# Attention scores from high and low halves in three one-pass products, roots of x for eight tiles at a time, and the last addition of q's rotation on GpSimd

## The reference

```python
q = rope(rmsnorm(q.reshape(B, L, N_HEADS, HEAD_DIM), q_norm_w), pos)
k = rope(rmsnorm(k.reshape(B, L, N_KV_HEADS, HEAD_DIM), k_norm_w), pos)
s = jnp.einsum('bnqkgd,bnskd->bnkgqs', qb, kc).astype(jnp.float32) / math.sqrt(HEAD_DIM)
p = sink_softmax(s, mask[None, :, None, None], sinks).astype(vc.dtype)
o = jnp.einsum('bnkgqs,bnskd->bnqkgd', p, vc)
```

## Time and profile before

| | before |
|---|---|
| median of three runs | 1855.61 us |
| profiled execution, own time | 1853.68 us |
| its span, first to last instruction | 1851.9 us |
| TensorE matmuls busy | 1766.0 us (95%) |
| TensorE weight loads busy | 1428.1 us (77%) |
| VectorE busy | 1230.6 us (66%) |
| ScalarE busy | 647.7 us (35%) |
| GpSimd busy | 428.7 us (23%) |
| mean granted TensorE clock | 0.974 of full speed |

### The profile page before, as it was taken

How to read it: one execution, slowest core, us unless ns; L and a number is a source line. 1 busy time by engine, 2 the same in 40 slices (tenths; PEclk the granted TensorE clock), 3 DMA queues, 4 the chain that set the end, 5 groups by cost and what they waited for, 6 DMA issues and landing times. The chain is left out here.

```text
span 1851.9 us, 26031 instructions
## 1 busy us (share of the span) xinstructions
PE 1766.0 (95%) x8822; PEld 1428.1 (77%) x8822; DVE 1230.6 (66%) x2862; ACT 647.7 (35%) x1682; POOL 428.7 (23%) x554
## 2 busy tenths in 40 slices
PE   5899999999999996999999997999979999999999
PEld 4677777777777774888888885777757888888886
DVE  5787888677877877666656535898646564566532
ACT  5454455445445445231122102454332212122210
POOL 1122222122222222000000034799701111111110
PEclk8999999999999997999999998999988999999999
DMA  7211221123221101333342043666564455354322
GB/s 254 83 61 61 69 82 61 61 63 117 102 87 64 38 25 55 103 96 134 100 143 78 24 152 98 161 173 165 127 146 116 108 131 159 117 136 113 117 92 65
DMA packets 198403, 191.61 MB, mean 103 GB/s; under 512 B 121344, under 2 KB 157184, under 8 KB 198272
## 3 DMA queue, kind: packets, MB, share of 16 engines
q1 hardware_dynamic: 187968, 181.53, 33.1%
q10 hardware_dynamic: 10304, 8.43, 2.2%
HBM read 130.81 MB, written 59.10 MB: 103 GB/s over the span
## 5 line engine op out<-in xcount | busy, mean ns | idle before, releaser
L1028 PE MATMUL ps_b<-b_WH,b_XH 128*128 128x512 f32 (+1 forms) x792 | 292.8, 370 | 18.7 <-DVE b_WL L1370 12.2
L1030 PE MATMUL ps_b<-b_WH,b_XL 128*128 128x512 f32 (+1 forms) x792 | 283.0, 357 | 0.0
L1029 PE MATMUL ps_b<-b_WL,b_XH 128*128 128x512 f32 (+1 forms) x792 | 282.8, 357 | 0.0
L1028 PEld LDWEIGHTS ps_b<-b_WH,b_XH 128*128 128x128 f32 x792 | 151.3, 191 | 48.4 <-issue 25.1
L1030 PEld LDWEIGHTS ps_b<-b_WH,b_XL 128*128 128x128 f32 x792 | 151.0, 191 | 22.2
L982 POOL TENSOR_TENSOR b_XL<-b_XT,b_XH 128x1024 fp32r<-128x1024 f32 x33 | 79.9, 2422 | 375.6 <-ACT b_XH L1200 316.8
L1029 PEld LDWEIGHTS ps_b<-b_WL,b_XH 128*128 128x128 f32 x792 | 151.7, 191 | 19.1
L1266 ACT ACTIVATE b_SM<-ps_b,b_small 128x128 f32<-128x128 f32 x256 | 113.7, 454 | 109.4 <-DVE b_small L1441 106.9
L674 PE MATMUL ps_e<-w_X0H,w_nextH 128*128 128x464 f32 x320 | 122.2, 382 | 1.6 <-DVEq L719 1.6
L676 PE MATMUL ps_e<-w_X0H,w_nextL 128*128 128x464 f32 x320 | 120.0, 375 | 0.0
L675 PE MATMUL ps_e<-w_X0L,w_nextH 128*128 128x464 f32 x320 | 119.7, 374 | 0.0
(11 more groups left out here) (316 smaller groups left out, 4084.6 us busy)
## 6 DMA issues: line engine op xcount, KB each, us to landing
b_XT<-in_xb SPq DMA_DIRECT2D x33, 512.0 KB
b_XR<-in_x SPq DMA_DIRECT2D x33, 512.0 KB, 4.7
w_XT<-in_xt SPq DMA_DIRECT2D x36, 464.0 KB, 7.2
l_X<-in_xr SPq DMA_DIRECT2D x32, 512.0 KB, 4.7
out_out<-l_OUT SPq DMA_DIRECT2D x32, 512.0 KB, 3.0
scr_gs<-e_TG SPq DMA_DIRECT2D x36, 232.0 KB, 2.0
scr_u<-w_ST SPq DMA_DIRECT2D x12, 696.0 KB, 3.7
g_U<-scr_u SPq DMA_DIRECT2D x192, 43.5 KB
```

The costliest lines, as they stand in the source:

```text
L1028: pe.matmul(bank[:, 0:c1 - c0], XH[b][:, k, :], WH[:, k, c0:c1], start=(k == 0), stop=False)
L1029: pe.matmul(bank[:, 0:c1 - c0], XH[b][:, k, :], WL[:, k, c0:c1], start=False, stop=False)
L1030: mm = pe.matmul(bank[:, 0:c1 - c0], XL[b][:, k, :], WH[:, k, c0:c1], start=False, stop=(k == KD - 1))
```

## The change

- Scores: QT and KT become pairs QTH, QTL and KTH, KTL of type fp32r. ScalarE writes the high halves (queries, keys), VectorE the low ones (new low_q, low_k), placed behind gate_attn(t). The 8 score matmuls of a tile become 24: high with high, low q with high k, high q with low k, into the same place in PSUM. TensorE waits for q's low half behind the first four and for k's behind the next four.
- Roots of x: x_rsqrt covers eight tiles and is called at t = 3, 11, 19, 27 instead of 3, 7, ..., 27. Loads and squares of x run ten tiles ahead instead of five, two a tile until t = 4.
- q's rotation: its addition moves from VectorE to GpSimd (rotated_q), between add_up(t-1) and low_x(t+2). k's stays on VectorE.
- Semaphore counts follow.

```diff
 def batch_of(t):
-    return 0 if t < 5 else (t - 5) // 4 + 1
+    return (t + 3) // 8
+
+def squares(t):
+    return range(t + 5 + min(t, 5), min(t + 6 + min(t + 1, 5), NT))
...
-                    if t + 5 < NT:
-                        load_xr(t + 5)
+                    for n in squares(t):
+                        load_xr(n)
...
+                def rotated_q(t):
+                    rope.wait(pool, tile(t), 3)
+                    pool.tensor_tensor(RQK[:, 0:DA], RQK[:, 0:DA], ZS[:, 0:DA], ALU.add).then_inc(q_rot, 1)
...
                 for t in range(NT):
                     if t >= 2:
                         add_up(t - 1)
+                    if t + 1 < NT:
+                        rotated_q(t + 1)
                     if t + 2 < NT:
                         low_x(t + 2)
                         tables(t + 2)
...
-                    for j in range(4):
-                        for g in HALVES:
-                            rows = slice(HD * g, HD * g + HD)
-                            mm = pe.matmul(ps[:, 4 + 2 * g + j // 2, 256 * (j % 2):256 * (j % 2) + 256], QT[rows, j, :], KT[rows, :, :],
-                                           start=True, stop=True)
-                            if j == 3:
-                                mm.then_inc(sc_full, 1)
+                    for i in range(2):
+                        for n, (q_, k_) in enumerate(((QTH, KTH), (QTL, KTH), (QTH, KTL))):
+                            if i == 0 and n == 1:
+                                pe.wait_ge(qT_lo, t)
+                            if i == 0 and n == 2:
+                                pe.wait_ge(kT_lo, t + 1)
+                            for j in (i, i + 2):
+                                for g in HALVES:
+                                    rows = slice(HD * g, HD * g + HD)
+                                    mm = pe.matmul(ps[:, 4 + 2 * g + j // 2, 256 * (j % 2):256 * (j % 2) + 256], q_[rows, j, :], k_[rows, :, :],
+                                                   start=(n == 0), stop=(n == 2))
+                                    if j == 3 and n == 2:
+                                        mm.then_inc(sc_full, 1)
...
                 def q_transposes(t):
-                    rope.wait(pe, tile(t), 4)
+                    pe.wait_ge(q_rot, t + 1)
...
                 def x_rsqrt(n):
-                    c = slice(0, 5) if n == 0 else slice(4 * n + 1, 4 * n + 5)
+                    c = slice(max(8 * n - 3, 0), min(8 * n + 5, NT))
...
+                    if part == 0:
+                        rope.mark(dve.tensor_tensor(r, z, cos, ALU.mult))
+                    else:
+                        rope.link(dve, tile(t), dve.tensor_tensor(r, z, cos, ALU.mult))
+                        rope.link(dve, tile(t), dve.tensor_tensor(RQK[:, c], RQK[:, c], ZS[:, c], ALU.add))
...
+                def low_q(t):
+                    dve.wait_ge(qT_out, t)
+                    if t >= 2:
+                        dve.wait_ge(sc_full, 2 * (t - 1))
+                    dve.tensor_tensor(QTL[:].rearrange("p j q -> p (j q)"), TB, QTH[:].rearrange("p j q -> p (j q)").bitcast(F32), ALU.subtract).then_inc(qT_lo, 1)
+
+                def low_k(t):
+                    dve.wait_ge(kT_out, t + 1)
+                    if t >= 2:
+                        dve.wait_ge(sc_full, 2 * (t - 1))
+                    dve.tensor_tensor(KTL[:, t % 2, :], KTB, KTH[:, t % 2, :].bitcast(F32), ALU.subtract).then_inc(kT_lo, 1)
...
                     if t:
                         gate_attn(t)
+                    if t + 1 < NT:
+                        low_q(t + 1)
+                        low_k(t + 1)
                     sample_softmax(t)
-                    if t % 4 == 3 and t < NT - 2:
-                        x_rsqrt((t + 1) // 4)
+                    if t % 8 == 3 and t < NT - 2:
+                        x_rsqrt((t + 5) // 8)
```

More of the change, by code:

```diff
@@ L809, in attention_tiles @@
         SQ = sb("SQ", [P, QK])
-        QT, KT = sb("QT", [P, 4, P]), sb("KT", [P, 2, P])
+        QTH, QTL = (sb("QT" + hl, [P, 4, P], F32R) for hl in "HL")
+        KTH, KTL = (sb("KT" + hl, [P, 2, P], F32R) for hl in "HL")
         VS = [sb(f"VS{i}", [P, P]) for i in range(3)]
@@ L855, in attention_tiles @@
         q_out, k_out, v_out, qk_sq = sem("q_out"), sem("k_out"), sem("v_out"), sem("qk_squared")
-        rope, chain = stage("rope_steps", 8), stage("qk_rsqrt", RS + 3)
+        q_rot, rope, chain = sem("q_rotated"), stage("rope_steps", 7), stage("qk_rsqrt", RS + 3)
         qT_full, kT_full, qT_out, kT_out = sem("qT_full"), sem("kT_full"), sem("qT_out"), sem("kT_out")
+        qT_lo, kT_lo = sem("qT_low"), sem("kT_low")
         sc_full, soft, exped = sem("scores_full"), stage("softmax_max", 10), stage("exped", 10)
@@ L987, in tables @@
                     if t >= 2:
-                        rope.wait(pool, tile(t - 2), 7)
+                        rope.wait(pool, tile(t - 2), 6)
                     for i in range(2):
@@ L1010, in _ @@
                 tables(1)
+                rotated_q(0)
                 for t in range(NT):
@@ L1041, in project_kv @@
                     if t:
-                        pe.wait_ge(kT_out, t)
+                        pe.wait_ge(kT_lo, t)
                     project(t, ZKV, DA, DA + 2 * P, kv_full)
@@ L1209, in copy_q @@
                     if t:
-                        rope.wait(act, prev(t), 7)
+                        rope.wait(act, prev(t), 6)
                         act.wait_ge(qk_sq, t)
@@ L1244, in queries @@
                         act.wait_ge(sc_full, 2 * (t - 1))
-                    act.activation(QT[:].rearrange("p j q -> p (j q)"), TB, ACT.Copy).then_inc(qT_out, 1)
+                    act.activation(QTH[:].rearrange("p j q -> p (j q)"), TB, ACT.Copy).then_inc(qT_out, 1)
                 def keys(t):
@@ L1250, in keys @@
                         act.wait_ge(sc_full, 2 * (t - 1))
-                    act.activation(KT[:, t % 2, :], KTB, ACT.Copy).then_inc(kT_out, 1)
+                    act.activation(KTH[:, t % 2, :], KTB, ACT.Copy).then_inc(kT_out, 1)
                 def gates(t):
@@ L1348, in _ @@
                         high_x(t + 2)
-                    if t + 5 < NT:
-                        square_x(t + 5)
+                    for n in squares(t):
+                        square_x(n)
                     if t + 1 < NT:
@@ L1392, in rotate @@
                         dve.wait_ge(tabs, 2 * t + 2)
+                        if t:
+                            dve.wait_ge(q_rot, t)
                         if t >= 2:
@@ L1398, in rotate @@
                     rope.mark(dve.tensor_tensor(s[:, :, 32:64], z[:, :, 0:32], sin[:, :, 32:64], ALU.mult))
-                    rope.link(dve, tile(t), dve.tensor_tensor(r, z, cos, ALU.mult))
-                    rope.link(dve, tile(t), dve.tensor_tensor(RQK[:, c], RQK[:, c], ZS[:, c], ALU.add))
+                    if part == 0:
[3 more added lines that the diff above has]
+                        rope.link(dve, tile(t), dve.tensor_tensor(RQK[:, c], RQK[:, c], ZS[:, c], ALU.add))
                 def norm_qk(t):
@@ L1413, in norm_qk @@
                     if t == 0:
+                        dve.wait_ge(q_rot, 1)
                         dve.tensor_tensor(heads(RQ0), heads(RQK[:, 0:DA]), bcast(RQS[:, 0:8], HD), ALU.mult).then_inc(kept, 1)
@@ L1520, in _ @@
                         rotate(t + 1, 0)
+                        if t == 0:
+                            low_k(0)
                         rotate(t + 1, 1)
```

## The result

The changed kernel takes 1872.57 us, the median of four runs (1870.87 to 1874.41); the kernel before, timed beside it, 1854.90 (four runs, 1851.81 to 1855.79). The ratio is 1.0094, 95% interval 1.0081 to 1.0106: slower, by 17.7 us. The forecast of 1871 and its sign hold. The profiled execution took 1871.56 us, its span is 1869.8, 17.9 more than before. One of the ten executions of the kernel with the roots alone took 5824 us; it is counted as slow and stays out of that kernel's ratio.

A forecast was written before the change was run, and what follows sets the result against it. TensorE, busy 20.32 of a plain tile's 20.5 us, was taken to set the period. Terms +1.3 + 15.6 - 4.3 + 0.6 + 3.2 = +16.4 us on 1853.7 gave 1870, stated as 1871 for the median; range 1853 to 1881.

The forecast's parts named there:

- its sign: Whole kernel: slower, given 0.73, against 0.15 for faster by over 0.2% and 0.12 for the same.
- Four long tiles: Tiles behind the four remaining root calls: k's rotation waits for GpSimd's addition and low_x, 4 x 3.9 = +15.6 us.
- roots: Calls of x_rsqrt, seven become four: 7 x 0.61 = 4.3 us removed; squares that run ahead cost nothing.
- Plain tiles: 25 plain tiles: wait for q's low half in the scores, +0.05 us each, +1.3 us together (-1 to +2).
- Start: Stretch before the scores of tile 1: the forecast had no cost there.
- The part on the low halves: low_q (0.68 us) and low_k (0.28) on VectorE, both within the 2.26 us in which it waited for scores.
- Tiles 1 and 2: In tile 1 k meets low_x again, a little earlier, by an estimated 0.4 us; counted in the rest of +0.6.
- Clock: Granted clock falls to the 1.2 GHz level behind long tiles: 0 to 6.4 us, two falls taken, +3.2.
- k's third product doesn't slip through: Rival, 0.20: three k products pass before GpSimd's addition, long tiles cost 8.4 us, no clock price: +6, 1862.
- the low halves do not arrive within the first four products: Rival, 0.13: low halves arrive in time, 0.29 us kept in each of 32 tiles, -9.3, total 1844.
- halves of the array take turns: Rival, 0.06: one-pass score products on the two array halves do not overlap, 32 x 1.2 = +38, 1900.

The follow-up runs named there:

- pair of second profiles: Changed kernel and kernel before, each run once more without an edit: 1876.41 us (ratio 1.0116) and 1854.84 us (ratio 0.9992).

## Why the prediction was right, and where it was not

The total came out within 2 us. The mechanism that decided the sign, k's rotation held behind GpSimd in the four tiles behind a root call, was the one forecast. The rest of the sum was not as good. The forecast put all of its +16.4 us into the tiles; in the profiled pair (17.9 us) they hold +8.8, and the start (+4.4) and the part behind the tiles (+4.7) the rest. By steps:

- **Four long tiles, +15.6, and roots, -4.3.** Right. Tiles 4, 12, 20, 28 are longer by 12.6 together, tiles 8, 16, 24 shorter by 1.4: +11.2 against +11.3. The cause was right for the changed kernel, down to the operation that is held. It was too narrow, though: the run with q's addition back shows that the later root call alone brings k into low_x, and the run with the addition alone shows that it does so without the low halves in four of seven tiles. So either of two parts of the change can make a tile long, and undoing the addition gives back almost nothing (1.0083 for 1.0094). The change without the scores, with roots by eight and the addition on GpSimd, was not run. What does give it back is the order between k's rotation and GpSimd's work.
- **Plain tiles, +0.05 each.** About right in size (20.47 to 20.55 or 20.56), wrong in the cause. The forecast put it on the wait for q's low half and called the addition's delay covered. Periods of 20.45 with scores alone, with q's addition undone and with GpSimd waiting for k, and 20.57 with q's addition alone, say that the 0.1 us is the addition's. VectorE in tile 18 of the changed kernel, then GpSimd:

```profile
444.07 0.68 DVE L1421 TENSOR_TENSOR b_RQK<-b_RAW,b_TAB 128x512 f32<-128x512 f32 x1
445.19 1.01 DVE L1418 TENSOR_TENSOR b_ZS<-b_RAW,b_TAB 128x64 f32<-128x64 f32 x1 [0.43 <-ACT b_RAW L1235]
...
444.83 1.28 POOL L1014 TENSOR_TENSOR b_RQK<-b_RQK,b_ZS 128x512 f32<-128x512 f32 x1 [8.21 <-DVE b_RQK L1421]
```

k's first product is held for 0.8, and split_probs starts 12.79 behind the scores instead of 12.33 (forecast +0.5). The forecast expected 0.2 to remain at gate_attn; what it overlooked is gate_of, ahead of gate_attn on VectorE. The last transposes before the scores wait for it ("0.23 <-DVE b_GATE" at 453.98), so the delay reaches the start of the scores and not low_q.
- **Start, nothing.** This failed. The part on the low halves priced low_k by the 2.26 us of idle time ahead of the maxima, where it stands in every tile but the first. Of low_k(0), which the diff places behind q's rotation, and of the wait in project_kv it said nothing. It cost 4.4 us in this pair: 2.6 of waiting, the rest from k and v projected at the lower clock. In the pair of second profiles it is 6.9. Moving low_k(0) ahead gave back 2.5.
- **Tiles 1 and 2, -0.4 named.** They gave back 3.6 (42.56 for 46.14), and it hid the miss at the start in the total. In the repeats the two tiles take 44.04 against 46.23. Of the 3.6, 1.5 is tile 2 (20.53 for 22.07), where the kernel before has a fall of the clock; the changed kernel has one in tile 1, from 62.1 to 65.5. The other 2.0 is tile 1, in which k meets the addition but slips past low_x. VectorE and GpSimd there, in the changed kernel:

```profile
74.04 1.39 DVE L1423 TENSOR_TENSOR b_RQK<-b_RAW,b_TAB 128x128 f32<-128x128 f32 x1
75.46 0.29 DVE L1424 TENSOR_TENSOR b_RQK<-b_RQK,b_ZS 128x128 f32<-128x128 f32 x1
...
75.53 2.49 POOL L988 TENSOR_TENSOR b_XL<-b_XT,b_XH 128x1024 fp32r<-128x1024 f32 x1 [0.26 <-ACT b_XH L1219]
```

low_x waits for ScalarE's high half, and k's last operation begins 0.07 us ahead of it. split_probs starts 14.4 behind the scores instead of 16.5. In the second profile low_x begins at 75.39 and k's last operation at 75.62; it is held for 2.38, split_probs starts at 15.9 and the tile takes 23.48. So this gain was luck by some tenths of a microsecond.
- **Clock, +3.2.** Right as a range (0 to 6.4), not as a sum. The first profile has no fall behind a long tile; the repeat has two, for 3.1 and 1.5 us.
- **Rest, not in the forecast:** the +4.7 behind the tiles is the spread from one profile to the next.
- **The rivals.** k's third product doesn't slip through, and the low halves do not arrive within the first four products. That halves of the array take turns is excluded by the 0.24 us of two pairs. The trace of the changed kernel now agrees, for one-pass products, with the Trainium skill (TensorEngine Tiling (Array Packing), Tiling Modes), by which different tiles of the array multiply in parallel: 0.12 us per pair, the time of one 256-column product by itself.
- **The working.** Three slips moved little. +16.4 on 1853.7 and 1.9 make 1872, not 1871. "25 plain tiles" counts all but the seven behind a root call; only 15 of the 31 periods before are 20.45 to 20.49 us, and tile 15 takes 30.54 (30.61 after). And with +38 the rival of halves in turn gives 1894, not 1900.

So the total was right partly by luck: misses of opposite sign met, +4.4 at the start and +4.7 behind the tiles against -3.2 for the clock and -3.2 more than forecast in tiles 1 and 2. The pair of second profiles shows it with other numbers: start +6.9, tiles +14.5, behind them +0.6, together 21.9. The long tiles, the term that decided the sign, were measured as they had been worked out, in both pairs.

## What to carry to other kernels

Before giving an engine more work, look not only for its idle time but for what then happens at the same moment on an engine it shares a resource with: here 1 us of delay, or 0.69 us less work on VectorE in exchange for 1.3 on GpSimd, cost 2.4 to 3.6 us in a tile, because an operation of 64 or 128 columns stood behind one of 2.4 us. The cure was an order, not less work: let the long GpSimd operations start when the short VectorE ones are through, beside work that reads PSUM. And look at the first iteration by itself: an operation placed for the steady state may stand elsewhere there, and a new reader of a PSUM bank delays whoever writes the bank next.

## What was unexpected of the hardware

- With GpSimd's addition and low_x back to back, a VectorE operation whose two inputs lie in SBUF can be held twice: in tile 20 of the changed kernel two begin before the addition does, at 487.87 and 488.01, the third waits for the addition and then gets through, and the fourth waits for low_x. The third and fourth together take 3.77 us instead of 0.57.
- An operation that is already late by 0.15 us is held for the full 2.4 (only the roots, tile 20). In tile 1 of the changed kernel one that was early by 0.07 us took 0.29. The edge is sharp, so the 1.8 us that three root calls fewer gave in tiles 8, 16 and 24 were lost in one tile (+2.3).
- Four one-pass products of 64 rows, two overlapping pairs, take 0.24 us: each pair takes the time of one 256-column product on all 128 rows.
- In the pause of 3.3 us at the start the granted clock fell to its lower level for 6.8 us. With k's first low half early and with the roots alone TensorE waits 2.5 us in two pieces there, and the clock fell for 3.4. Behind the long tiles, in which TensorE idles for as much (24.40 less 20.84), it fell in some tiles of some profiles and not in others. What decides that is open.
